# A hybrid attention block on one core: four gate halves move into the projection stage, query stores and loads are recut

## The reference, cut to what matters

```python
mod = silu(c) @ w_ada + b_ada                       # sh1, sc1, gt1, sh2, sc2, gt2
h = rms_norm(x, g_pre_mix) * (1 + sc1) + sh1
proj = h @ w_in   # q 512 | 6 x 128 keys and values | 24 gates | 512 pooled channels u | 2048 merge gates br_g
q = rope(q); kc_c = compress(rope(kc)); vc_c = compress(vc)   # 32-token blocks, stride 16, two small products, gelu
o_nsa = nsa_attention(...)        # per 128 queries: selected, window (512) and compressed keys, three softmaxes
o_pool = pool_mixer(u)            # causal means over 2, 4, 8, 16 tokens, per-group product
gate_a, gate_b = split(sigmoid(br_g))
merged = gate_a * (o_nsa @ w_br_nsa) + gate_b * (o_pool @ w_br_pool)
x = x + gt1 * rms_norm(merged @ w_out, g_post_mix)
# then a squared-ReLU MLP (1024 -> 4096 -> 1024) with sh2, sc2, gt2
```

## Time and profile before

| | us |
|---|---|
| median of 3 runs (lowest, highest) | 1481.42 (1477.32, 1482.05) |
| the profiled execution | 1481.94 |
| its span | 1480.1 |
| projection block 4 begins | 124.11 |
| attention begins | 256.99 |

### The profile page before, as it was taken

One profiled execution on the slowest core, in us unless ns is written; L12 is line 12 of the kernel. 1 busy time (PEld: TensorE's weight loads), 2 busy tenths in 40 slices (PEclk: granted clock), 3 DMA queues, 4 the chain that ended last, 5 costly groups with the idle time before them and its releaser, 6 DMA issues.

```text
span 1480.1 us, 19531 instructions
## 1 busy us (share of the span) xinstructions
PE 1412.2 (95%) x7206; PEld 1181.4 (80%) x7206; DVE 1074.1 (73%) x1483; ACT 636.9 (43%) x1112; POOL 331.0 (22%) x429
## 2 busy tenths in 40 slices
PE   2897999999999999989999999999999999999997
PEld 2886878888888888868887877888888888888885
DVE  6668854677777878885441789777777797777778
ACT  1534433556665666663122664222222434343342
POOL 3323422333322322111210410000000030404034
PEclk9998999999999999999999999999999999999999
DMA  9378945322121111015453424544443773535226
GB/s 352 80 242 256 275 110 165 99 64 74 56 70 36 55 60 42 19 63 181 146 184 110 142 72 148 207 157 149 144 150 135 275 285 113 199 106 206 88 84 227
DMA packets 130854, 208.31 MB, mean 141 GB/s; under 512 B 19653, under 2 KB 84677, under 8 KB 127175
## 3 DMA queue, kind: packets, MB, share of 16 engines
q1 hardware_dynamic: 127178, 196.61, 40.4%
q0 software_dynamic: 3584, 10.49, 2.1%
HBM read 146.24 MB, written 54.53 MB: 136 GB/s over the span
## 4 chain that ended last, share of the span: by engine, by line
PE 80%; DVE 10%; issue 3%; ACT 3%; SPq 2%; DMA 1%; POOL 0%; DVEq 0%; POOLq 0%; ACTq 0%
PE ps L2060 18%; PE ps L2062 17%; PE ps L2061 17%; PE ps L2066 5%; PE ps L2068 5%; PE ps L2067 5%; PE ps L2255 4%; PE ps L2271 2%; PE ps L2222 2%; PE ps L2272 2%; PE ps L2223 2%; DVE acc L1548 1%; DVE ada_acc L1421 1%; SPq L538 1%; DVE pt_lo L1604 1%
## 5 line engine op out<-in xcount | busy, mean ns | idle before, releaser
L2060 PE MATMUL ps<-act_hi,a_hi 128*128 128x512 f32 x448 | 191.7, 428 | 2.2 <-DVE a_lo L1400 2.2
L2062 PE MATMUL ps<-act_hi,a_lo 128*128 128x512 f32 x448 | 176.3, 394 | 0.0
L2061 PE MATMUL ps<-act_lo,a_hi 128*128 128x512 f32 x448 | 175.9, 393 | 0.0
L2060 PE MATMUL ps<-wr_hi,left_hi 128*128 128x512 f32 x320 | 124.5, 389 | 0.0
L2061 PE MATMUL ps<-wr_lo,left_hi 128*128 128x512 f32 x320 | 124.5, 389 | 0.0
L2062 PE MATMUL ps<-wr_hi,left_lo 128*128 128x512 f32 x320 | 124.5, 389 | 0.0
L1604 DVE TENSOR_TENSOR pt_lo<-ps,pt_hi 128x512 fp32r<-128x512 f32 (+1 forms) x160 | 103.0, 644 | 20.1 <-ACT pt_hi L1139 18.7
L1321 ACT ACTIVATE left_hi<-left_st 128x2048 fp32r<-128x2048 f32 x28 | 53.6, 1916 | 144.9 <-PE ps L2062 81.5
L1241 ACT ACTIVATE w_hi<-w1s 128x1024 fp32r<-128x1024 f32 x54 | 57.0, 1057 | 112.3 <-PE ps L2062 74.8
L1139 ACT ACTIVATE pt_hi<-ps 128x512 fp32r<-128x512 f32 (+1 forms) x160 | 89.0, 563 | 32.8 <-PE ps L2255 31.1
L1728 DVE TENSOR_TENSOR w_lo<-w1s,w_hi 128x1024 fp32r<-128x1024 f32 x54 | 65.9, 1222 | 51.1 <-ACT w_hi L1241 51.0
(11 more groups left out here) (279 smaller groups left out, 3872.1 us busy)
## 6 DMA issues: line engine op xcount, KB each, us to landing
left_st<-h_dram SPq DMA_DIRECT2D x28, 1024.0 KB, 5.0
ada<-in_w_ada SPq DMA_DIRECT2D x48, 512.0 KB, 5.8
h_dram<-hid SPq DMA_DIRECT2D x48, 512.0 KB, 3.1
w1s<-in_w_fc SPq DMA_DIRECT2D x32, 512.0 KB, 4.2
w2s<-in_w_fc SPq DMA_DIRECT2D x16, 1024.0 KB, 7.9
raw<-in_w_in SPq DMA_DIRECT2D x28, 512.0 KB, 4.2
g_dram<-g_out POOLq DMA_DIRECT2D x32, 256.0 KB, 2.4
mg<-g_dram SPq DMA_DIRECT2D x16, 512.0 KB, 3.9
```

The lines of the kernel that those rows point to most:

```text
L2060: pe.matmul(dst, wh, mh, start=start, stop=False)
L2061: pe.matmul(dst, wh, ml, start=False, stop=False)
L2062: return pe.matmul(dst, wl, mh, start=False, stop=stop)
```

## The change

Four gate halves (`EARLY`) move to the projection stage. The weight stream's order is now the list `STREAM`, with the first gate block at position 5 and the second at 9; `AT` gives a block's position. TensorE makes halves 0 and 1 after block 4 (before `compress(0)`), half 2 after block 7, then the first part of the second modulation, half 3, and its second part. These four go through one buffer `g_early`: each tanh waits for the store before it. After block 11 come halves 4 and 5. Halves 6 to 30 go to iterations 0 to 32 without 10, 13, 16, 19, 22, 25, 28 and 31. Query stores become two full-width DMAs per half, `q_dram` gets a new layout, and a chunk's load becomes two DMAs of 512-byte rows.

```diff
-HALF_OF = {half - 2: half for half in range(2, HALVES - 1)}
+EARLY = 4
+UNFILLED = (10, 13, 16, 19, 22, 25, 28, 31)
+HALF_OF = dict(zip([it for it in range(UNITS + 1) if it not in UNFILLED], range(EARLY + 2, HALVES - 1)))
+UNIT_OF = {half: it for it, half in HALF_OF.items()}
+STREAM = [0, 1, 2, 3, 4, N_FM, 5, 6, 7, N_FM + 1, 8, 9, 10, 11] + list(range(N_FM + 2, N_FM + N_BR))
+AT = {w: p for p, w in enumerate(STREAM)}
+GATE_BANKS = (7, 5, 5, 7, 7, 6)
...
-    K_DMAS, Q_DMAS = 8, 4
+    K_DMAS, Q_DMAS = 8, 2
...  (SyncE)
+                if a in Q_BLOCKS:
+                    h = 2 * (a - Q_BLOCKS[0])
+                    for x, part in enumerate((r_hi, r_lo)):
+                        sp.dma_start(q_dram[x, h:h + 2, :, ch * CH:(ch + 1) * CH].rearrange("g d n -> (g d) n"),
+                                     full(part[:, i % 2, :])).then_inc(rope_out[i % 2], 16)
+                    continue
...
-            if a:
+            if a and a < 10:
                 load_fm(a + 1)
+            if a in (9, 10):
+                load_fm(a + 2)
...
-            if a == 6:
+            if a == 7:
                 cmp_load(1)
...
-            sp.dma_start(full(q_st[:, c % 2, :, :]), q_dram[c]).then_inc(pair_in[c % 2], 16)
+            for x in range(2):
+                sp.dma_start(full(q_st[64 * x:64 * x + 64, c % 2, :, :]),
+                             q_dram[x, :, :, c * P:(c + 1) * P].rearrange("h d q -> d h q")).then_inc(pair_in[c % 2], 16)
 
         load_fm(N_FM + 1)
         mix_store(0)
+        load_fm(N_FM + 2)
         load_q(0)
         load_q(1)
         mix_store(1)
-        for m in range(2, N_BR):
+        load_fm(N_FM + 3)
+        mix_store(2)
+        mix_store(3)
+        c = 2
+        for m in range(4, N_BR):
             load_fm(N_FM + m)
-            if m == 2:
-                mix_store(2)
-                mix_store(3)
-            if m % 2 == 1 and m >= 5:
-                load_q(m // 2)
+            while c < TT and (m == N_BR - 1 or UNIT_OF.get(2 * (m - 2), 0) > 4 * c - 4):
+                load_q(c)
+                c += 1
...  (GpSimd)
         for a, k in FM_ROPE.items():
+            if a == 5:
+                gate_store(0)
+                gate_store(1)
...
+        gate_store(2)
+        gate_store(3)
...  (ScalarE)
+            if 1 <= h < EARLY:
+                act.wait_ge(g_st[(h - 1) % 2], 16 * ((h - 1) // 2 + 1))
...
-            split_a(a + 2)
+            split_a(AT[a] + 2)
+            if a == 4:
+                gate_evict(0)
+                gate_evict(1)
+            if a == 7:
+                gate_evict(2)
+                gate_evict(3)
+            if a in (4, 7):
+                split_a(AT[a] + 3)
...  (VectorE)
-            split_a(a + 2)
+            split_a(AT[a] + 2)
...
+            if a in (4, 7):
+                split_a(AT[a] + 3)
...  (TensorE)
+            if f == 0:
+                pe.wait_ge(ada2_added, 4 * KT)
+                pe.wait_ge(gate_tanh, 3)
...
             if a == 4:
+                gate_part(0, range(KT))
+                gate_part(1, range(KT))
                 compress(0)
             if a == 6:
                 compress(1)
             if a == 7:
-                second_modulation()
+                gate_part(2, range(KT))
+                second_modulation(0)
+                gate_part(3, range(KT))
+                second_modulation(1)
```

More of the change, by code:

```diff
@@ L451, in load_fm @@
         def load_fm(a):
[L453 removed]
+            f = FM_COLS[STREAM[a]]
+            load_raw(R_FM + a, parts=((raw_k(R_FM + a), w_in_v[:, :, f:f + P]),))
         def ada_piece(n):
@@ L510, in rope_stores @@
                         src = full(part[64 * g:64 * g + 64, i % 2, :])
[L511 to L519, removed]
+                        for half in range(2):
+                            rows, row = slice(64 * half, 64 * half + 64), 2 * (a - K_BLOCKS[0]) + g
+                            sp.dma_start(full(kd[rows, row, ch * CH:(ch + 1) * CH]), src).then_inc(rope_out[i % 2], 16)
         def cmp_load(kv):
@@ L830, in _, with gate_store @@
         pool.wait_ge(cos_in, 32)
+        def gate_store(h):
+            m = h // 2
+            pool.wait_ge(gate_tanh, h + 1)
+            pool.dma_start(g_dram[m // KT, m % KT, h % 2], g_early[:, :] if h < EARLY else g_out[:, h % 2, :]) \
+                .then_inc(g_st[h % 2], 16)
         for a, k in FM_ROPE.items():
+            if a == 5:
+                gate_store(0)
+                gate_store(1)
             for ch in range(2):
@@ L880, in split_gate_block @@
                                ALU.subtract).then_inc(lo_done, 1)
-        gate_store(0)
-        gate_store(1)
+        gate_store(EARLY)
+        gate_store(EARLY + 1)
         for it in range(UNITS + 1):
@@ L960, in split_a @@
             if a >= 2:
-                free = (fm_mm, 2 * a - 2) if a - 2 < N_FM else (gate_mm, 2 * (a - 2 - N_FM) + 2)
+                w = STREAM[a - 2]
+                free = (fm_mm, 2 * w + 2) if w < N_FM else (gate_mm, 2 * (w - N_FM) + 2)
             split_hi(R_FM + a, a_hi[:, a % 2, :], free)
@@ L1052, in cmp_store, with gate_evict @@
                            ACT.Copy).then_inc(cmp_hi, 1)
+        def gate_evict(h):
+            act.wait_ge(gate_mm, h + 1)
+            if 1 <= h < EARLY:
+                act.wait_ge(g_st[(h - 1) % 2], 16 * ((h - 1) // 2 + 1))
+            elif h >= 2:
+                act.wait_ge(g_st[h % 2], 16 * (h // 2))
+            act.activation(g_early[:, :] if h < EARLY else g_out[:, h % 2, :], ps[:, gate_bank(h), :], ACT.Tanh, scale=0.5) \
+                .then_inc(gate_tanh, 1)
         def pooled_hi_part(g):
@@ L1094, in _ @@
                 mix_evict(a - 9)
[L1096 to L1104, removed]
+        gate_evict(EARLY)
+        gate_evict(EARLY + 1)
         mix_evict(3)
@@ L2122, in project @@
                 w = slice(k * P, (k + 1) * P)
-                ins = three(ps[:, bank, :], a_hi[:, a % 2, w], a_lo[:, a % 2, w], act_hi[:, k, sl], act_lo[:, k, sl],
+                ins = three(ps[:, bank, :], a_hi[:, AT[a] % 2, w], a_lo[:, AT[a] % 2, w], act_hi[:, k, sl], act_lo[:, k, sl],
                             k == 0, k == KT - 1)
@@ L2152, in mix, with second_modulation @@
                     .then_inc(mix_mm, 1)
[L2154 to L2169, removed]
+        def second_modulation(f):
+            if f == 0:
+                pe.wait_ge(ada2_added, 4 * KT)
+                pe.wait_ge(gate_tanh, 3)
+            for half in range(2):
+                if f:
+                    pe.wait_ge(gt_row, half + 1)
+                pe.matmul(ps[0:1, 4 + half, :], ones[:, 0:1], acc2[:, 3 * f, half * CH:(half + 1) * CH],
+                          start=True, stop=True).then_inc(gt_mm, 1)
+            if f == 0:
+                for n in range(16):
+                    ins = pe.matmul(ps[:, 7, n:n + 1], acc2[:, 1 + n // KT, (n % KT) * P:(n % KT + 1) * P],
+                                    ones[:, 0:1], start=True, stop=True)
+                ins.then_inc(mod2_mm, 1)
         def gate_part(h, ks):
             if 0 in ks:
-                pe.wait_ge(lo_done, R_FM + N_FM + h // 2 + 1)
-                if h >= 2:
+                pe.wait_ge(lo_done, R_FM + AT[N_FM + h // 2] + 1)
+                if h < 2:
+                    pe.wait_ge(v_lo, TT)
+                    pe.wait_ge(v_hi, 2 * TT)
+                elif h == 3:
+                    pe.wait_ge(mod_done, 4)
+                else:
                     pe.wait_ge(gate_tanh, h)
-            ins = project(N_FM + h // 2, 6 if h == 1 else 7, h % 2, ks)
+            ins = project(N_FM + h // 2, gate_bank(h), h % 2, ks)
             if KT - 1 in ks:
@@ L2201, in _ @@
         pe.wait_ge(mod_done, 4)
-        gate_part(0, range(KT))
+        gate_part(EARLY, range(KT))
         pe.wait_ge(cmp_lo, 3)
-        gate_part(1, range(KT))
+        gate_part(EARLY + 1, range(KT))
         mix(3)
```

19 lines of the change are left out of this document (9 added, 10 removed).

## The result

The changed kernel takes **1531.45 us** (median of 4 runs, 1529.58 to 1532.93) against 1481.16 (1477.32 to 1482.05): ratio **1.0333**, 95% interval 1.0319 to 1.0348. That is 50 us more, where 31 were forecast, and outside the range of 1488 to 1522.

A forecast was written before the change was run, and what follows sets the result against it. TensorE, busy 95% of the span, was taken to bound the kernel, with VectorE right behind in attention. Start of attention +35.1, first split +2.5, attention -6.6: +31 us on 1481.9, less 0.5 for the median, gives 1512 us, range 1488 to 1522.

The forecast's parts named there:

- Two gates: 288.7: After block 11: two gate halves run until 288.7 us, then 2.0 us idle for the last pooling before the last mix.
- The second compression: Projection stage: TensorE idles 4.5 us before it, it runs partly at half clock, done at 182.5 us (before: 174.5).
- The second modulation and gate half 3: Before block 8: 3.2 us idle, modulation 5.5 + 0.5, gate 3 with slow start 6.5, last columns 1.9, until 216.5.
- Rival D: Stalls longer than forecast, each bringing half-clock matmuls: +40 us, 1522; chance 0.11.
- The mixes: Late projection stage: first mix waits 1.9 us, second 9.2 us behind late loads and pooling; block 11 has 1.8 slow clock.
- The first split in attention: Its load stands behind the last mix's store; ScalarE is held 4.2 us, gate pieces cover some, cost 2.5 us.
- Attention: Seven iterations losing a gate half save 12.1 us, three gaining one cost 5.5: net 6.6 us saved.
- Undisturbed: Attention: iterations without a gate half have VectorE's smaller busy time, free of the GpSimd split; 7.99 us for iteration 10.
- the rival of 3 us more: Attention: VectorE's excess stays with the iteration, three of the seven save some 3 us less; no chance given.
- A: Early part as worked out, but late loads ahead of attention don't bite: +13.5 us, 1495; chance 0.22.
- C: Perfect filling, and attention's unfilled iterations run at VectorE's bare busy time: -7 us, 1475; chance 0.05.
- B: Perfect filling of TensorE's idle time in the projection stage, no new stall: +2.9 us, 1485; chance 0.07.

The follow-up runs named there:

- run 1: The changed kernel, but gate half 5 no longer waits for the tanh of an earlier half: 1522.86 us, ratio 1.0278 to the kernel before.
- run 4: The changed kernel without gate half 5's wait, weight and gate loads ahead of stores, second compression's load back in its old turn: 1499.1 us, ratio 1.0113.
- run 7: On top of run 4, VectorE's four block additions for the second compression placed ahead of the weight split: 1490.06 us, ratio 1.0048.
- run 5: On top of run 4, the four early gate halves stored by ScalarE's queue instead of GpSimd's: 1496.4 us, ratio 1.0104.
- run 2: The changed kernel, with the weight loads for the two last projection blocks' positions issued ahead of the key stores: 1519.83 us, ratio 1.0250.
- run 3: The changed kernel, with the two gate weight loads issued ahead of the second, third and fourth mix's stores: 1525.85 us, ratio 1.0287.
- run 10: The kernel before with the changed kernel's attention stage, four gate halves' products left out altogether: 1475.73 us, ratio 0.9960.
- run 8: On top of run 7, early halves stored by ScalarE's queue, weight loads ahead of modulation loads from block 6's turn on: 1487.66 us, ratio 1.0038.
- run 12: As run 8, but only two early halves, behind block 4, and attention's last six iterations without a gate half: 1477.43 us, ratio 0.9961 to the kernel before.

## Why the prediction was right in direction and wrong in size

Forecast 1512 with 1488 to 1522, measured 1531.5. Right: slower, for the stated reason, with the stalls in the places named before the compression, the modulation and the second mix. Wrong by 19.4 us, and no single term explains it (run 1, without the largest, takes 1522.86). Term by term:

- **The step that failed is "Two gates: 288.7", in part 3.** It took gate half 5 to follow half 4 at once and put 2.0 us of idle time before the last mix. Half 5 waits for half 4's tanh, which stands on ScalarE behind the last pooling, and lost 7.96 us idle and 2.9 us of slow clock: 10.9 for 2.0, 8.9 too few. Run 1 takes this wait alone away and gains 8.6 to 10.0. The prediction counted every load's place in the queue, and not that a moved half changes its number, on which a wait hangs.
- **The second compression,** 3.8 us too small: done at 186.3, forecast 182.5. The blocks' data was 1.4 later than 173.7, the additions took 4.69 instead of 3.8, the matmuls 6.47 where the forecast's 182.5 leaves 5.0 (its own 5.5 would have given 183.0). It named the one-buffer tanh, the load a turn late and the additions' length. The data did come last here, as it said. With the load back in its turn (run 4) the gap stayed at 6.25, since now the additions' place behind a split came last, which the prediction did not see (run 7); there the tanh carries little (run 5). What it carries in the changed kernel, where the late load stands behind query stores that wait for ScalarE, was not tried.
- **The second modulation and gate half 3,** 5.2 too small: 19.65 us from its start to block 8, forecast 14.4. The forecast put the modulation at full clock after a 3.2 us wait; after 2.64 us the clock was 0.53 for ten microseconds. Rival D had this mechanism, with too small a price. No run removes the slow clock behind this gap by itself.
- **The mixes:** gaps of 0.87 and 8.19 for 1.9 and 9.2, and 2.3 of slow clock for 1.8. This step held; run 2 confirms its cause.
- **The first split in attention,** +5.7 for +2.5. ScalarE is held 5.11 us. The scores wait for ScalarE as well, 2.55 and 1.31 us, so the gate pieces cover little, and from 322 to 326 the clock is 0.56 to 0.58, some 2 us more that the forecast left out. Run 3 gives it all back.
- **Attention,** -6.6 as forecast, but by terms that cancel. The seven iterations take 81.2 us for the 84.5 forecast, so they save 15.6 (96.8 before, at exact cuts) and not 12.1; iterations 29, 30 and 32 cost 5.0 for 5.5; and 4.0 us of longer neighbours, 2.2 of them in iteration 17, were in no step of the forecast. "Undisturbed" was right: VectorE is busy 7.91 us in iteration 10 now, and the one behind it, which has the GpSimd split, 9.71 (9.60 in the earlier trace rows when it was iteration 10's). The Trainium skill's rule on contention (GPSIMD Engine Reference, section Specifications) agrees with that, and the rival of 3 us more is out.

Of the rivals, A (late loads don't bite) fell with run 2, C with run 10. B, perfect filling at +2.9, is nearly what run 8 reaches, at +5.2: the stage's floor was right to 2.3 us (+11.8 for +9.5), and the change as it stands was 45 us above run 8.

## What to carry to other kernels

Moving work earlier into an in-order stream moves everything keyed to its place: its weight load on the DMA queue, the split behind it, and waits that hang on its number; list each queue's order anew and look for what now stands behind stores or behind another engine's late turn. Moved work costs its own length less the idle and slow time that it fills, and gains what its old place gives back. Count both before choosing how much to move: here two halves cost 1.0 us in the new place and gave back 4.7 in the old one, a gain of 0.4% by the ratio; four, with their stalls taken away (run 8), cost 11.8 and gave back 6.5. Where a gap is left, price the matmuls behind it at half speed.

## What the runs showed that was not expected

- The price of the slow clock varied between runs of the same order of work: the 32 small matmuls of the modulation took 6.99 us here and in run 3, 4.24 in run 1 and 4.06 in run 2, after gaps of 2.64, 3.73, 3.18 and 3.10 us; 4.92 in run 7 after 1.85. The gap's length alone does not order them. Nor is it that the slow clock only falls elsewhere: from the modulation's first matmul to gate half 3 these first four take 10.3, 10.9, 7.9 and 7.9 us. What orders them was not tried.
- An iteration behind an unfilled one can be slower though TensorE never waits in it. Iteration 17 took 16.24 us instead of 14.07, busy all the time, with the granted clock down to 0.74 in part of it; the other successors grew by 0.6 at most. Runs 4 and 10 have the same at iteration 17 (the first row below, of run 10), with 1.1 to 1.2 us more at iteration 11 as well. But in runs 3, 7 and 8 most of it falls on iteration 11, which takes 13.09, 13.99 and 13.11 instead of 11.13, and iteration 17 only 14.64. The idle pieces in iteration 10, 1.15, 0.99, 0.73 and 0.23 us, are the same to 0.02 in run 3 and in the changed kernel, and yet the next three microseconds ran at 0.65 in the one and at 1.00 in the other (the second and third row). So the idle time of the iteration ahead does not settle it.

```profile
434.50:450.70 16.20, 16.20 (x103) 14.22 (x102) 11.64 (x24) 9.18 (x21) 4.25 (x8) 0.92 0.14 36
```

```profile
415.00:418.00 3.00, 3.00 (x14) 2.51 (x13) 2.14 (x6) 1.60 (x5) 0.85 (x2) 0.65 0.10 22
```

```profile
421.00:424.00 3.00, 3.00 (x19) 2.44 (x18) 2.81 (x8) 2.65 (x6) 0.85 (x3) 1.00 0.10 22
```

- Two more unfilled iterations side by side, 27 and 28 in run 12, saved 3.9 us with no longer neighbour, 1.95 each; the seven spread ones saved 15.6 less 4.0, 1.7 each. That is not a gain of standing side by side: 2.2 of the 4.0 are iteration 17's slow clock, and without it the spread ones save 2.0 each too.
